# Odd attention: the middle tile of an iteration with three tiles, moved in front of the mixing

## The reference, cut to what matters

```python
def stick_breaking(q, k, v):
    scale = q.shape[-1] ** -0.5
    for i in range(L // BLOCK):
        s, e = i * BLOCK, (i + 1) * BLOCK
        z = jnp.einsum('bqhd,bkhd->bhqk', q[:, s:e], k[:, :e]) * scale
        mask = (jnp.arange(e)[None, :] < jnp.arange(s, e)[:, None])[None, None]
        log_1m = jnp.where(mask, jax.nn.log_sigmoid(-z), 0.0)
        rest = lax.cumsum(log_1m, axis=3, reverse=True) - log_1m
        a = jnp.where(mask, jnp.exp(jax.nn.log_sigmoid(z) + rest), 0.0)
        outs.append(jnp.einsum('bhqk,bkhd->bqhd', a, v[:, :e]))

def odd_mixer(h, w_in, w_out):
    q, k, v = jnp.split(h @ w_in, 3, axis=-1)      # 16 heads of 64
    return stick_breaking(heads(q), heads(k), heads(v)).reshape(...) @ w_out
```

## Time and profile before

| | us |
|---|---|
| median of 3 runs | 2318.66 (2314.61 to 2318.88) |
| the profiled execution, its own time | 2321.87 |
| its span, first to last instruction | 2320.1 |
| TensorE busy in it | 2230.5 (96%) |
| mean granted TensorE clock | 0.979 |
| iterations 1 to 12 of the attention | about 1644 to 1857 |

### The profile page before, as it was taken

The page is one execution under the profiler, slowest core; times in us unless marked ns, Lnnn a source line. Parts: engine busy times, 40 slices in busy tenths (PEclk is TensorE's granted clock), DMA queues, the critical chain, the costliest instruction groups (busy, mean ns, idle before and its releaser), DMA issues. The chain is left out here.

```text
span 2320.1 us, 35416 instructions
## 1 busy us (share of the span) xinstructions
PE 2230.5 (96%) x14804; PEld 1979.7 (85%) x14804; DVE 1118.0 (48%) x1677; ACT 971.5 (42%) x1411; POOL 621.3 (27%) x480
## 2 busy tenths in 40 slices
PE   7999999998999999998999999999999999999998
PEld 5887578886589987886899999999988989988987
DVE  2348625557452234896444424444555534433443
ACT  5336644356534435335433313334555533322322
POOL 2012320113213424336123302322333212310321
PEclk9999999999999989989999999999999989999999
DMA  5442023210122212130233233222111013324322
GB/s 177 138 134 62 2 73 102 91 56 5 37 79 92 73 47 73 53 114 1 58 97 92 75 102 107 80 76 91 37 55 55 19 55 91 91 78 113 91 81 74
DMA packets 235215, 175.64 MB, mean 76 GB/s; under 512 B 7732, under 2 KB 230060, under 8 KB 234544
## 3 DMA queue, kind: packets, MB, share of 16 engines
q1 hardware_dynamic: 235056, 173.37, 25.0%
HBM read 171.20 MB, written 10.09 MB: 78 GB/s over the span
## 5 line engine op out<-in xcount | busy, mean ns | idle before, releaser
L334 DVE TENSOR_TENSOR panel_lo<-panel_raw,panel_hi 128x2048 fp32r<-128x2048 f32 (+2 forms) x148 | 325.6, 2200 | 280.9 <-ACT panel_hi L326 280.9
L326 ACT ACTIVATE panel_hi<-panel_raw 128x2048 fp32r<-128x2048 f32 (+2 forms) x151 | 268.3, 1777 | 370.9 <-PE product L432 256.6
L432 PE MATMUL product<-scaled_hi,panel_hi 128*128 128x272 f32 (+2 forms) x1232 | 282.4, 299 | 2.6 <-PEq L488 1.4
L432 PE MATMUL product<-scaled_lo,panel_hi 128*128 128x272 f32 (+2 forms) x1232 | 283.0, 299 | 0.0
L432 PE MATMUL product<-scaled_hi,panel_lo 128*128 128x272 f32 (+2 forms) x1232 | 282.8, 299 | 0.0
L432 PEld LDWEIGHTS product<-scaled_hi,panel_hi 128*128 128x128 f32 x1232 | 196.5, 188 | 11.8 <-issue 2.9
L432 PEld LDWEIGHTS product<-scaled_hi,panel_lo 128*128 128x128 f32 x1232 | 195.4, 188 | 7.5
L432 PEld LDWEIGHTS product<-scaled_lo,panel_hi 128*128 128x128 f32 x1232 | 194.5, 188 | 6.7
L445 PE MATMUL product_banks<-panel_hi,scaled_hi 128*128 128x256 f32 x696 | 193.8, 278 | 0.0
L445 PE MATMUL product_banks<-panel_lo,scaled_hi 128*128 128x256 f32 x696 | 193.7, 278 | 0.0
L445 PE MATMUL product_banks<-panel_hi,scaled_lo 128*128 128x256 f32 x696 | 193.6, 278 | 0.0
(11 more groups left out here) (584 smaller groups left out, 5437.3 us busy)
## 6 DMA issues: line engine op xcount, KB each, us to landing
panel_raw<-in_w_in_dram SPq DMA_DIRECT2D x26, 1024.0 KB, 5.3
panel_raw<-in_ffn_w_gate_dram SPq DMA_DIRECT2D x44, 512.0 KB, 4.0
panel_raw<-in_ffn_w_up_dram SPq DMA_DIRECT2D x44, 512.0 KB, 5.3
panel_raw<-in_ffn_w_down_dram SPq DMA_DIRECT2D x32, 704.0 KB, 4.7
panel_raw<-in_even_w_in_dram SPq DMA_DIRECT2D x21, 1024.0 KB, 5.2
panel_raw<-in_odd_w_in_dram SPq DMA_DIRECT2D x12, 1024.0 KB, 5.2
panel_raw<-in_w_out_dram SPq DMA_DIRECT2D x8, 1024.0 KB, 6.4
panel_raw<-in_even_w_out_dram SPq DMA_DIRECT2D x8, 768.0 KB, 4.9
```

Of the source, the lines that this page charges most:

```text
L326: act.activation(c.hi[g % 2][:, 0:used], c.raw[g % 2][:, 0:used], ACT.Copy).then_inc(c.hi_made.sem, 1)
L334: dve.tensor_tensor(c.lo[g % 2][:, 0:used], c.raw[g % 2][:, 0:used], c.hi[g % 2][:, 0:used].bitcast(F32), ALU.subtract).then_inc(c.lo_made ...
L432: done = pe.matmul(banks[b], weight(w, k), a[:, k, u:v], start=(k == 0 and x == 0), stop=(k == chunks - 1 and x == 2))
```

## The change

In the iterations that have three tiles, the middle one goes to slot AFTER_REST instead of AFTER_MIX:

```diff
         for h in range(GROUP * group - 3, GROUP * group + 1):
             for slot in (AFTER_FIRST, AFTER_REST, AFTER_MIX, AFTER_SCORE):
-                if slot != AFTER_REST or h == GROUP * group - 3:
+                if slot != AFTER_MIX or h == GROUP * group - 3:
                     PLAN[h, slot] = (n,)
                     n += 1
```

## The result

| | before | after |
|---|---|---|
| median, 20 runs each | 2322.24 us (2314.36 to 2327.88) | 2328.01 us (2318.83 to 2330.80) |
| ratio | | 1.0027 (95%: 1.0018 to 1.0036) |
| the profiled execution, its own time | 2321.87 | 2328.18 |
| its span | 2320.1 | 2326.4 |
| from the mixing of iteration 1 to that of iteration 13 | 204.38 | 208.43 |

The change makes the kernel slower by 0.27%, about 6 us; forecast were 2.6 us and no visible difference. I call it *the stretch*: it holds all nine changed iterations, TensorE's clock is at its full level throughout, and in two profiles of the changed kernel it came out as 208.43 and 208.38 us.

The account below looks back on a forecast made before the run. TensorE was taken to bound the kernel, with nothing to fill. Waits of +3.0 us and seams of -0.4 us gave +2.6 us on 2318.66, so 2321.3 us (+0.11%), range 2317 to 2327.5.

Parts of the forecast that it names:

- What bounds the kernel: TensorE, busy 96% of the span, has nothing to fill in the nine changed iterations; reordering gains only at seams or short waits.
- Iterations 3, 7 and 11: First V tile waits for DVE's `panel_lo`, no longer covered by the mixing: 0.99 us each, 3.0 us in all.
- The other covers: Q's second half in iterations 2, 6, 10, fresh tiles before the mixing's last pair, DVE's `result` copies: all cost nothing.
- The seams: Sums' start to scores' start in each changed iteration: 7.49 us becomes 7.44, -0.05 each, -0.4 us in all.
- From the sum to a time: The +2.6 us carried over to the median of before, 2318.66, giving 2321.3 us, +0.11%.
- A: Rival: in iteration 3 POOL's `plus_lo` takes the shared port before DVE's low part; waits of 3.0 us, 2327 us; 5%.
- B: Rival: `result` copies also delay the second bank's `soft`, each Ln and V tiles behind it; +4 us more, 2325.5; 4%.
- C: Rival: TensorE's clock falls in the new waits; +5 to +23 us, most likely about 2330; 5%.
- D: Rival: no loss, as the wait is covered, seams give more or short waits vanish; -0.4 to -2 us; 12%.

Follow-up runs that it names:

- early_low: The changed kernel with ACT and DVE splitting the V panel one iteration earlier (iterations 2, 6, 10): 2319.53 us, ratio 1.0003 to before.
- others_only: The kernel before with the new order only in iterations 2, 4, 6, 8, 10, 12, the old one in 3, 7, 11: 2322.91 us, ratio 1.0012.
- tail_before: The kernel before with ACT's and POOL's step for the last head's key one iteration earlier: 2319.88 us, ratio 1.0006.
- tail_filled: tail_before plus four products that nobody reads on TensorE in front of the last head's sums: 2317.74 us, ratio 0.9985 to before.
- after_again: The changed kernel run once more, unaltered: 2324.30 us, ratio 1.0020 to before.
- v_tile_only: The kernel before with the middle tile in front of the mixing only in iterations 3, 7 and 11: 2324.09 us, ratio 1.0015.
- wide_last_after: The changed kernel with every mixing's matmuls in reverse order, 16-column ones first and the 512-column one last: 2325.11 us, ratio 1.0015 to before.
- tail_after: The changed kernel with the last head's key step one iteration earlier, as in tail_before: 2324.66 us, ratio 1.0018 to before.
- split_mixing: The kernel before with the AFTER_MIX tile of iterations 1 to 12 set into the middle of the mixing: 2327.81 us, ratio 1.0033.

## Why the prediction was right or wrong

**What bounds the kernel: right.** TensorE was full, so nothing was to be gained, and the loss is where a tile is asked for before its inputs.

**Iterations 3, 7 and 11: right in place, cause and size.** Forecast 0.99 us each, at the first V tile, for `panel_lo`, three times and nowhere else; measured 0.98 (0.99 in iterations 7 and 11), and early_low shows that nothing else was waited for.

**The other covers: right.** No wait in iterations 2, 6, 10 or for `wait_taken`; `result` delays only the first `soft` (1.56 us behind the scores, forecast 1.5).

**The seams: this step failed.** Forecast -0.4 us in all with bounds of -1.4 and +0.5; measured about +0.9 to +1.0 (0.10 to 0.11 x 9). Two things were wrong in it. The gain of 0.05 us for each iteration isn't there: from the sums' start to the scores' start iteration 2 takes 1.90 + 3.00 + 2.57 = 7.47 us after (forecast 7.44), but 1.97 + 2.57 + 2.93 = 7.47 before as well (and iteration 4, with a V tile, 7.48 both times). The 7.49 that it was set against is of iteration 3 with its V tile, and the 7.44 was put together with a Q tile of iteration 1. And the sum ended a matmul too early. A seam is also paid between the first and the second matmul of a group, and scores behind a tile don't pay it, while scores behind a mixing do: 0.10 us. It should have been closed at the start of the group behind the scores. That is 1.3 to 1.4 us, and it takes the forecast from +2.6 to 3.9 or 4.0 of the stretch's +4.05, just beyond its bound of 3.8.

**From the sum to a time: this failed too.** I set +2.6 on 2318.66, the median of three runs that spread over 4.3 us. With 20 runs before stands at 2322.24, 3.6 us higher. Of the 6.7 us between the forecast of 2321.3 and the measured 2328.01, 3.6 are this base, 1.4 are the seams, and 1.7 are more than the stretch holds and stay open. So the base, more than the seams, put the time beyond 2327.5. The range had been made from the cases of the change, with too little for the place of the base itself.

**The rivals.** A didn't occur, though DVE's lead over POOL shrank from 0.08 to 0.03 us in iteration 3. The two did not keep their distance as exactly as I had argued: most of the lead was gone, so this was close. POOL's 4.15 us are 2.12 more than the 2.03 it takes alone in iteration 2, and DVE, which was first, still had 2.26 us to go when POOL started. The Trainium skill (SBUF — State Buffer, section SBUF: two separate sides) says that the port pair shared by DVE and GpSimd belongs for a whole instruction to the one that starts first; these rows agree with it again. B is refuted by others_only. C didn't occur: the clock is 1.00 over the stretch. The low clock that the profiles do show near the change is in the tail, which the change doesn't touch. D is refuted.

**Open.** The first comparison gave 6 us, the second 5, the trace 4.05. Whether the 1 to 2 us between belong to the change, by way of the tail's clock, or to chance isn't settled. Nor is why leaving the mixing costs 0.10 us.

## What to carry to other kernels

When a tile is moved forward, ask first whether it is the first user of something that another engine makes in the same iteration; the step that it is moved in front of may have been its cover, and the cost is then the distance between two rows that the trace already has. When groups of matmuls change places, measure from the start of one group to the start of the group behind the last one that moved, since a seam can cost inside the following group. And before a few microseconds are set on a base, look at how far the base itself moves from run to run.

## What the runs showed of the hardware

The low clock in the tail cost 4 to 5 us, more than either wait there (2.2 and 3.5 us). In tail_before the work behind the wait of 3.5 us ran at a mean granted clock of 0.53 over 11 us, of the two levels 1.2 and 2.4 GHz almost wholly the lower; in tail_filled, with four dead products in the wait (2.85 us of it), the clock stayed at 1.00, and the same 107 matmuls took 4.15 us less. The same waits don't always bring the low clock: early_low stayed at 1.00 with 2.2 and 3.5 us unfilled. The waits of 0.98 us in the middle of dense work never did, in five profiles with three each (after, after_again, v_tile_only, wide_last_after, tail_after: 1.00 over every stretch).

Leaving the mixing (matmuls on 64 columns of weights) costs TensorE 0.10 us, seen in the second matmul of the group behind it, whether the mixing's last matmul has 16 columns (0.33 instead of 0.23) or 512 (0.34). Entering it from a tile costs 0.09 us (split_mixing, 3.22 instead of 3.13), and setting a tile into its middle 0.35 us in all. A tile's second matmul comes 0.08 us late behind sums that end in 16 columns (0.20) and not behind sums that end in 400 (0.12).

POOL's `plus_lo` of 2.03 us takes 4.15 when DVE's `panel_lo` starts 0.03 us ahead of it, while that takes 2.29 as ever (after, iteration 3).
